# Two half-tiles of tokens in one gather, and their weighted sums through 128x64 diagonals side by side on TensorE

## The reference

```
def peer_ffn(xn, w_query, sub_keys, expert_u, expert_v):
    ...
    idx = i1 * PEER_N_KEYS + i2
    g = jax.nn.softmax(cv, axis=-1)
    ...
    def block(args):
        xb, ib, gb = args
        hid = jax.nn.gelu(jnp.einsum('td,thkd->thk', xb, expert_u[ib]).astype(jnp.float32), approximate=False)
        return jnp.einsum('thk,thkd->td', (gb * hid).astype(xb.dtype), expert_v[ib])
```

## Time and profile before

| | |
|---|---|
| median of 3 runs | 4050.73 us (4046.65 to 4053.82) |
| span of the profiled execution | 5878.7 us |
| its own time beside the span | none is given |
| instructions | 40315 |
| mean granted TensorE clock | 0.555 |
| busy: TensorE, VectorE, ScalarE, GpSimd | 5726, 2887, 1648, 1285 us |
| moved by DMA | 1444 MB, 246 GB/s over the span |

### The profile page before, as it was taken

How to read it: one execution, slowest core, us unless ns; L and a number is a source line. 1 busy time by engine, 2 the same in 40 slices (tenths; PEclk the granted TensorE clock), 3 DMA queues, 4 the chain that set the end, 5 groups by cost and what they waited for, 6 DMA issues and landing times.

```text
span 5878.7 us, 40315 instructions
## 1 busy us (share of the span) xinstructions
PE 5726.4 (97%) x13374; PEld 2787.7 (47%) x13374; DVE 2887.4 (49%) x5745; ACT 1648.5 (28%) x4216; POOL 1285.3 (22%) x1094
## 2 busy tenths in 40 slices
PE   9999999999999998999999999899999999899999
PEld 5555555444444545444445545344445555222222
DVE  3321003665555455756555555756555554744443
ACT  3431101344422211244432211245422211222222
POOL 0000000222222221322222221322222221334343
PEclk6555555555555555555555555555555555555555
DMA  4222222767777775767777775777777775899997
GB/s 155 93 102 81 73 90 95 267 238 266 261 275 268 274 280 202 285 245 280 273 272 297 283 291 190 280 256 271 271 268 308 281 290 191 315 350 342 345 342 281
DMA packets 212948, 1444.45 MB, mean 246 GB/s; under 512 B 27256, under 2 KB 27256, under 8 KB 46340
## 3 DMA queue, kind: packets, MB, share of 16 engines
q0 software_dynamic: 164976, 1133.94, 52.0%
q1 hardware_dynamic: 47632, 307.80, 14.4%
q10 hardware_dynamic: 132, 0.12, 0.0%
HBM read 1439.31 MB, written 7.13 MB: 246 GB/s over the span
## 4 chain that ended last, share of the span: by engine, by line
PE 96%; DVE 2%; ACT 1%; issue 1%; DMA 0%; SPq 0%; ACTq 0%; DVEq 0%
PE banks L609 52%; PE sums L871 21%; PE banks L871 7%; PE banks L748 5%; PE banks L827 3%; PE banks L669 2%; PE banks L736 1%; PE banks L786 1%; PE banks L778 1%; PE banks L694 1%; PE banks L844 1%; DVE x L1479 1%; DVE rows L1470 0%; PE banks L637 0%; PE banks L700 0%
## 5 line engine op out<-in xcount | busy, mean ns | idle before, releaser
L609 PE MATMUL banks<-hT,ring 128*128 128x256 f32 x6656 | 2608.4, 583 | 4.7 <-DVE arena L1316 3.9
L609 PEld LDWEIGHTS banks<-hT,ring 128*128 128x128 f32 x6656 | 1507.5, 228 | 1151.7 <-issue 734.0
L576 POOL DMA_INDIRECT rows<-in_w_uv,idx x1024 | 1237.6, 1209 | 3600.3 <-PE sums L871 1981.3
L1470 DVE CUSTOM_DVE_ANT_0 rows<-rows,xn 128x1024 f32<-128x1024 f32 x1024 | 1241.6, 1220 | 530.8 <-DMA rows<-in_w_uv,idx 528.0
L871 PE MATMUL sums<-rows,diag 128*128 128x512 f32 x1612 | 1285.2, 970 | 70.0 <-ACT diag L1076 47.9
L1479 DVE SCALAR_TENSOR_TENSOR x<-rows,wgt,x 128x1024 f32<-128x1024 f32 x493 | 632.0, 1282 | 234.8 <-ACT wgt L1068 234.0
L871 PEld LDWEIGHTS sums<-rows,diag 128*128 128x128 f32 x1612 | 369.2, 232 | 791.7 <-issue 683.2
L1281 DVE SCALAR_TENSOR_TENSOR arena<-banks,pr,arena 128x254 f32<-128x254 f32 (+1 forms) x512 | 246.8, 482 | 354.6 <-ACT arena L965 340.9
L1063 ACT ACTIVATE gelu<-hid 128x2 f32<-128x2 f32 x512 | 102.9, 201 | 1100.7 <-DVE hid L1470 1099.3
L609 PE MATMUL banks<-yT,ring 128*128 128x256 f32 x1024 | 400.2, 582 | 0.0
L871 PE MATMUL banks<-rows,diag 128*128 128x512 f32 x512 | 393.7, 966 | 0.0
(11 more groups left out here) (205 smaller groups left out, 2955.8 us busy)
## 6 DMA issues: line engine op xcount, KB each, us to landing
ring<-in_w_ssd SPq DMA_DIRECT2D x96, 1024.0 KB, 5.4
ring<-in_w_att SPq DMA_DIRECT2D x64, 1024.0 KB, 6.1
ring<-in_w_mrg SPq DMA_DIRECT2D x52, 1024.0 KB, 8.4
arena<-a_rows POOLq DMA_DIRECT2D x32, 1024.0 KB, 7.6
ring<-in_w_qry SPq DMA_DIRECT2D x32, 1024.0 KB, 4.8
arena<-bias_tiles POOLq DMA_DIRECT2D x16, 1152.0 KB, 7.3
ring<-in_w_out SPq DMA_DIRECT2D x16, 1024.0 KB, 7.0
rows<-in_w_uv,idx POOLq DMA_INDIRECT x1024, 6.8
```

The source lines that it names most:

```text
L576: nc.gpsimd.indirect_dma_start(out=rows[n % NB][:, :], out_offset=None, in_=w_uv, in_offset=bass.IndirectOffsetOnAxis(ap=idx[:, t, s:s + 1 ...
L609: mm = pe.matmul(out, w[:, k * P:(k + 1) * P], rhs[:, k0 + k, :], start=start and k == 0, stop=stop and k == n - 1)
L1470: v.tensor_tensor_reduce(u, u, xn2[:, (n // SLOTS_T) % 3, :], 1.0, 0.0, ALU.mult, ALU.add, hid[:, k:k + 1]).then_inc(u_done, 1)
```

## The change

Tokens are dealt differently over partitions. A gather used to bring one slot of a tile's 128 tokens. Now slots go in pairs, and gather q of a pair (q = 0, 1) brings both slots for 64 tokens, those of half q of the tile: partitions 0 to 63 have one slot, 64 to 127 another (its index is 8 further in the head). So `idx`, `gate` and the normalized x (`xn2`) are laid out by half: `xn2` holds each half's 64 tokens twice, once on each half of the partitions. VectorE writes each half's own copy (`own_rows`) and ScalarE the other (`copies`). The second tile's copies are made in the ssd stage of the next pass (`late_rows`). The norm weight is loaded straight into `xn2` by half tiles, without the wait for the finished x.

The dot product stays one VectorE instruction of 128x1024 a gather. The sum of a pair is now four matmuls, for each 512 columns two: the diagonal is 128x64, two 64x64 diagonals stacked, so that both slots of a token are added in the contraction, and gather q goes to output partitions 64q to 64q + 63. No sum is on VectorE any more. The sum of a pair stands at the even tick k, for slots k - 4 and k - 3. `hid`, `gelu` and `wgt` shrink to 16 columns, `DIAGS` goes from 5 to 6. Gathers are as many and as large as before.

```diff
-BESIDE = [("norm", 0, 1, 8, 60), ("ssd", 0, 2, 22, 80), ("ssd", 2, GROUPS, 70, 50), ("att", 0, 4, 65, 15), ("mrg", 0, 8, 42, 5),
-          ("out", 0, 1, 11, 0), ("norm2", 0, 1, 5, 100), ("query", 0, 2 * PH + 1, 13, 0), ("route", 0, REST, 20, 100)]
+BESIDE = [("norm", 0, 1, 8), ("ssd", 0, 2, 22), ("ssd", 2, GROUPS, 68), ("att", 0, 4, 68), ("mrg", 0, 8, 47),
+          ("out", 0, 1, 11), ("norm2", 0, 1, 5), ("query", 0, 2 * PH + 1, 12), ("route", 0, REST, 15)]
...
-    return list(range(SLOTS_P - LAG - 1, SLOTS_P)) if k == SLOTS_P - 1 else [k - LAG] if k >= LAG else []
+def sums_at(k):
+
+    if k == SLOTS_P - 1:
+        return list(range((k - LAG) // 2, PAIRS_P))
+    return [(k - LAG - 1) // 2] if k % 2 == 0 and k > LAG else []
...
+    c[:, C_I64:C_I64 + HALF] = i[:, None] % HALF == i[None, :HALF]
...
-        xn2 = sb("xn2", [P, 3, D])
+        xn2 = sb("xn2", [P, 2, 2, D])
...
-        diag = [sb(f"diag{n}", [P, P]) for n in range(DIAGS)]
+        hid = sb("hid", [P, HID])
+        diag = [sb(f"diag{n}", [P, HALF]) for n in range(DIAGS)]
...
-                yield place("norm2", 0, 0.2)
-                pool.wait_ge(x_mid.sem, x_mid.at(m, 2))
-                pool.dma_start(n2b, w_n2[m // 2].partition_broadcast(P)).then_inc(n2_in.sem, 16)
+            def norm_rows(m, t):
+
+                for q in range(2):
+                    pool.dma_start(xn2[HALF * q:HALF * q + HALF, t, q, :],
+                                   w_n2[m // 2].partition_broadcast(HALF)).then_inc(n2_in.sem, 16)
...
                     for h in range(2):
-                        mm = pe.matmul(sum_banks(p, t)[:, h, :], diag[e % DIAGS][:, :],
-                                       rows[n % NB][:, D + 512 * h:D + 512 * h + 512], start=q == mine[0], stop=q == mine[-1])
+                        for q in range(2):
+                            mm = pe.matmul(sum_banks(p, t)[HALF * q:HALF * q + HALF, h, :], diag[(2 * n + q) % DIAGS][:, :],
+                                           rows[(2 * n + q) % NB][:, D + 512 * h:D + 512 * h + 512],
+                                           start=j % PAIRS_T == 0, stop=j % PAIRS_T == PAIRS_T - 1)
                     mm.then_inc(v_pe, 1)
...
+            def copies(m, t):
+
+                act.wait_ge(xn_own.sem, xn_own.at(m, t + 1))
+                for q in range(2):
+                    own, other = HALF * q, HALF * (1 - q)
+                    ins = act.activation(xn2[other:other + HALF, t, q, :], xn2[own:own + HALF, t, q, :], ACT.Copy)
+                ins.then_inc(xn_ok.sem, 1)
...
+                for q in range(2):
+                    act.wait_ge(g_w, n + q)
+                    act.activation(diag[(n - 1 + q) % DIAGS][:, :], stacked, ACT.Copy, scale=wgt[:, c + q:c + q + 1]).then_inc(d_ok, 1)
...
+            def own_rows(m, t, scale):
+
+                v.wait_ge(n2_in.sem, n2_in.at(m, 32 * (t + 1)))
+                for q in range(2):
+                    at = slice(HALF * q, HALF * q + HALF)
+                    ins = v.scalar_tensor_tensor(out=xn2[at, t, q, :], in0=x[at, 2 * (m % 2) + t, :], scalar=scale[at],
+                                                 in1=xn2[at, t, q, :], op0=ALU.mult, op1=ALU.mult)
+                ins.then_inc(xn_own.sem, 1)
...
-                    v.scalar_tensor_tensor(out=xo, in0=rows[before % NB][:, D:], scalar=wgt[:, q:q + 1], in1=xo,
-                                           op0=ALU.mult, op1=ALU.add).then_inc(v_dve, 1)
+                v.tensor_tensor_reduce(u, u, xn2[:, t, q, :], 1.0, 0.0, ALU.mult, ALU.add,
+                                       hid[:, n % HID:n % HID + 1]).then_inc(u_done, 1)
```

More of the change, by code:

```diff
@@ L80 @@
 AHEAD = NB - LAG - 1
-DIAGS = 5
+DIAGS = 6
+HALF = P // 2
+PAIRS_T = SLOTS_T // 2
+PAIRS_P = SLOTS_P // 2
+HID = 16
 BEHIND = 3.0
@@ L103, in part_of @@
     return next(n for n, (m, tile, lo, hi) in enumerate(PARTS) if (m, tile) == (p, t) and lo <= h < hi)
-BESIDE = [("norm", 0, 1, 8, 60), ("ssd", 0, 2, 22, 80), ("ssd", 2, GROUPS, 70, 50), ("att", 0, 4, 65, 15), ("mrg", 0, 8, 42, 5),
-          ("out", 0, 1, 11, 0), ("norm2", 0, 1, 5, 100), ("query", 0, 2 * PH + 1, 13, 0), ("route", 0, REST, 20, 100)]
-LAST_ON_DVE = 3
-EARLY = [("query", 14, 17, 3, 100), ("route", 0, REST, 7, 100)]
+BESIDE = [("norm", 0, 1, 8), ("ssd", 0, 2, 22), ("ssd", 2, GROUPS, 68), ("att", 0, 4, 68), ("mrg", 0, 8, 47),
+          ("out", 0, 1, 11), ("norm2", 0, 1, 5), ("query", 0, 2 * PH + 1, 12), ("route", 0, REST, 15)]
+EARLY = [("query", 14, 17, 3), ("route", 0, REST, 7)]
 FEWER = {"ssd": 4, "att": 4, "mrg": 2}
 def deal(table):
-    return [(AT[phase] + EACH[phase] * (first + (last - first) * (i + 1) / ticks),
-             (i + 1) * percent // 100 > i * percent // 100) for phase, first, last, ticks, percent in table for i in range(ticks)]
-BESIDE_1 = [(name, lo, hi, n - (FEWER.get(name, 0) if lo != 0 or name != "ssd" else 0), q) for name, lo, hi, n, q in BESIDE]
+    return [AT[phase] + EACH[phase] * (first + (last - first) * (i + 1) / ticks)
+            for phase, first, last, ticks in table for i in range(ticks)]
+BESIDE_1 = [(name, lo, hi, n - (FEWER.get(name, 0) if lo != 0 or name != "ssd" else 0)) for name, lo, hi, n in BESIDE]
 DEALT = [deal(EARLY), deal(BESIDE_1)] + [deal(BESIDE)] * (PASSES - 2)
 assert len(DEALT[0]) + len(DEALT[1]) == len(DEALT[2]) == SLOTS_P
[L123 to L126, removed]
+PLAN = [[(0, k, due) for k, due in enumerate(DEALT[0])],
+        [(0, len(DEALT[0]) + k, due) for k, due in enumerate(DEALT[1])]]
+PLAN += [[(m - 1, k, due) for k, due in enumerate(DEALT[m])] for m in range(2, PASSES)]
 EARLY_AT = 12
@@ L537, in decay_rows @@
                     pool.dma_start(aBC.rearrange("p d h t -> p d (h t)"), src).then_inc(bc_in.sem, 16)
+                if m:
+                    yield place("ssd", 0, 0.3)
+                    late_norm_rows(m - 1)
                 yield place("ssd", 0, 0.5)
@@ L966, in mixer @@
                                        scale=pr[:, o + 2:o + 3]).then_inc(c_acc.sem, 1)
+                    if m and g == 1:
+                        yield place("ssd", g, 0.7)
+                        copies(m - 1, 1)
                     if m and g == LATE_STEPS - 1:
```

146 lines of the change are left out of this document (70 added, 76 removed).

## The result

The changed kernel takes 4140.5 us (median of 4 runs, 4135.4 to 4142.2) against 4050.9 for the one before: a ratio of 1.0222, 95% interval 1.0208 to 1.0237. It is slower by 90 us.

What follows compares the result with a forecast made beforehand. At the full clock DMA was taken to bound most of the kernel, VectorE close behind. From 4051 us, 27 for three passes and 18 of a 55 us excess came off: 4006, said as 4005, range 3890 to 4190.

Steps and rivals of the forecast that it cites:

- The timed runs are at the full clock: Whole kernel: the first case, timed runs at 2.4 GHz and not the profile's 0.555, so mostly DMA's.
- pass of 909 us: Third pass of the kernel before: the largest of TensorE, VectorE and DMA time in each stage, added up.
- VectorE's 766 us a pass fall by 210: Passes: sums leave VectorE, leaving about 560 us; largest terms fall 9 us a pass, plus 18 us in all given back.
- A pair costs what one slot costs: Sums on TensorE: four half-width matmuls, two side by side, take one slot's 1.71 us at 2.4 GHz; +62 us a pass.
- 0.15 for the visit: TensorE going in and out of half width: 0.15 us for each of 384 pairs, bounds 0 and 0.2; +19 us a pass.
- TensorE stays under DMA: Att and mrg after the change: TensorE needs 213 us of DMA's 233 in att, 187 of 199 in mrg.
- TensorE becomes the bound: Rival in att and mrg: the added sums make TensorE decide below a granted clock of 0.93; 4150 us, chance 0.20.
- Late gathers: Rival: even slots' sums come one tick later, so gathers have 4 ticks instead of 5; 4084 us, chance 0.12.
- No change: Rival: DMA covers all and the 9 us a pass are within the rate's error; 4051 us, chance 0.13.
- halves don't run together: Rival on TensorE: a pair's two halves run one after the other; over 5000 us timed, chance 0.01.
- ScalarE's diagonals 0.34 us: ScalarE: 1024 diagonals of 128x64 instead of 531 of 128x128, 0.34 us each, +140 us in all, hidden.
- no gain in the last stretch at the full clock: Last pass, only gathers: TensorE's time per slot halves, but at the full clock DMA already set it, so nothing.

Runs made afterwards that it cites:

- r9: Kernel before with VectorE's sums done on 8 of their 1024 columns, nothing put on TensorE: 3973.7 us, ratio 0.9807.
- r6: Changed kernel with the sum of a pair one tick earlier, so each buffer is free sooner: 4145.1 us, ratio 1.0236.
- r5: Kernel before with half of the att and mrg sums on TensorE, as single full-width slots: 4111.3 us, ratio 1.0150.
- r4: Changed kernel with half of the output columns of nearly all sums left out on TensorE: 4080.4 us, ratio 1.0071.
- r2: Changed kernel with the tick counts by stage of the kernel before: 4144.5 us, ratio 1.0237.
- r10: Changed kernel with two pairs summed per visit to half width, only for ticks 104 to 223 (about att and mrg): 4128.3 us, ratio 1.0188.
- r7: Changed kernel with two pairs summed per visit to half width everywhere, at every fourth tick: 4189.6 us, ratio 1.0341.
- r1_base: Kernel before, unchanged, run again for a profile at the full clock: 4043.8 us.

## Why the prediction was wrong

It said 4005, faster than 4051. Measured are 4140: inside its range of 3890 to 4190, but on the other side. Step by step:

1. *The timed runs are at the full clock, and DMA bounds att and mrg there.* Right: clocks of 0.94 to 0.95 in every timed run of the kernel before, 416 and 425 GB/s, 71% of mrg's chain. Its pass of 909 us measured 914; that these are so close is in part luck, since the stages in it were cut wrongly (4.) and the rate was too low.
2. *VectorE's 766 us a pass fall by 210, and this frees time.* Right, and too cautious in size: I gave 9 + 6 us a pass for it, r9 shows 25 (76 us over the kernel).
3. *A pair costs what one slot costs, 1.71 us at 2.4 GHz, and 0.15 for the visit.* The first half is right: two 64-column records start 7 ns apart, and a step of the two takes 429 ns, as one of full width does. The price of the visit was too low: 0.35 us at the full clock, above the upper bound of 0.2 that I gave. In the trace ahead of the prediction, at a clock of 0.555, the same count over all steps around the heads gives 0.21 (median of ten), so in that trace a part of the price didn't show. The Trainium skill ("TensorEngine Tiling (Array Packing)", Key Properties) says that a change of tiling mode drains TensorE. The trace agrees that it costs, with 0.14 us on the way in and 0.20 on the way out, each less than the 0.38 us that a record of 256 columns lasts.
4. *TensorE stays under DMA: 213 of 233 us in att, 187 of 199 in mrg.* **This step failed.** Measured are 232 busy of 244, and 176 of 176, while DMA would need, at 425 GB/s, 222 us for att's 94.4 MB and 166 for mrg's 70.4. Four terms of it were mis-sized.
   - *The rate.* I took 400 GB/s for the limit, from a range whose upper end, 427, stood in the earlier trace rows: 11 us too many for DMA in att and 12 in mrg.
   - *The ends of the stages.* The stretches of the earlier trace rows don't end where the stages do. The trace has the last product of att (L786) and the first projection of mrg (L609) at 3256 us, not at 3223, and mrg's end at 3481. So 33 us of att were counted as mrg. With the right ends mrg has 64 MB and 125 us of TensorE at 2.4 GHz, where I had 74 and 148. By my own terms for the change, that is 164 us of TensorE against 162 of DMA at 427 GB/s: no room at all.
   - *The bytes.* At the full clock mrg of the kernel before had 56.5 MB, not 64: what a stage takes in changes with the clock. And the change brought it 13.9 MB more, where I had 5 gathers, 5.2 MB. The two nearly cancel.
   - *TensorE's own load.* In att the kernel before has 194 us busy at a clock of 0.94, which is 183 at the full one, where I had 172; and the visits cost 20 us in the two stages, not 9.

   So the room of 32 us in the two stages was not there. The rows for the ends, of the execution that the earlier trace rows are from: TensorE around 3256, and busy time by stretch as there, for att and mrg with their true ends:

```profile
3251.81 4.71 PE L786 MATMUL banks<-arena 128*64 128x256 f32 x24
3256.46 5.93 PE L609 MATMUL banks<-hT,ring 128*128 128x256 f32 x15
...
2935.00:3256.50 321.50, 317.73 (x865) 158.41 (x863) 179.09 (x266) 92.48 (x241) 87.09 (x70) 0.55 0.74 283
3256.50:3481.00 224.50, 224.50 (x583) 131.16 (x582) 109.53 (x153) 52.83 (x109) 52.94 (x42) 0.56 0.76 284
```

5. *The rival "TensorE becomes the bound", 4150, decides from a granted clock under 0.93.* The mechanism and its place were right. Its condition was wrong: 400 us of TensorE against 432 of DMA should have read 408 against 388. By that it happens at the full clock (0.98 to 1.00 in the two stages), and it should have been the forecast. Its price, 4150 against 4140 measured, was worked out from a clock of about 0.89 that no timed run had: that it came so near is luck.
6. *Late gathers* (4084): VectorE's waits for gathers did grow, 514 to 913 us, but r6 took back 251 of them for nothing, and r9 has 880 in a faster kernel. *No change* and *halves don't run together* fell.
7. *ScalarE's diagonals 0.34 us, VectorE near 2270, ScalarE near 1810, no gain in the last stretch at the full clock.* Measured 0.340, 2323, 1716, and 7 us gained.

The balance of a pass, by the shortfalls: att +17, mrg +10 and out to query +6, against -6 in ssd and -3 in route and norm. Shown by a run: that TensorE's load alone produces mrg's loss and, at 10 us less of it, over a third of att's, and makes the whole 61 us slower (r5), that its removal returns mrg's (r4), and that VectorE's relief alone is a gain (r9). Not settled is the rest of att's loss. Most of it stays when TensorE is relieved (r4), is not due to the counts or to the sum's tick (r2, r6), and a part of it goes with fewer visits (r10: 22 to 16). What remains of the change there is that buffers come free two at a time, and the visits, each of which holds up what stands behind it by 0.35 us; no run tells the two apart, since r7 and r10 change both. Nor was a mixture tried, pairs for one tile of a pass and the old sums for the other. No version that computes everything beat the kernel before.

## What to carry to other kernels

When two engines stand close, moving work pays only up to the second engine's limit in the very stage where it lands, so write for each stage the second engine's load beside the transfer time at the *best* rate the trace shows, since a rate taken too low makes room that isn't there. Find where a stage ends by its first and last instruction before counting its bytes: here 33 us of one stage, counted as the next, made a room of 12 us that wasn't there. Take the bytes and slots of a stage only from an execution in the regime of the timed runs: when a profile is 1.45 times as long as they are, stages have shifted against each other, and scaling one engine's time does not put them back. Read the price of a switch over a whole period, from one steady step to the next: reading its first steps alone gave 0.19 us for 0.35. A long wait on an engine is a price only if that engine ends last: VectorE's 900 us of waiting for gathers stood in the changed kernel and in the fastest one alike.

## What the runs showed of the hardware

- **A DMA share near 1 is not a full rate.** Mrg shows 1.01 at 425 GB/s in `r1_base` and 1.00 at 400 in the changed kernel, 1.00 at 399 in r5. The Trainium skill says that for DMA utilization of HBM, rather than occupancy, is to be read ("Perfetto Trace Analysis", Identifying the Most-Contended Engine); the trace agrees.
- **Going to half width for a pair and back costs TensorE 0.35 us.** At the full clock, f32, 128x64 between records of 128x128: 0.14 us on the way in and 0.20 on the way out, the same in 33 of 34 visits between projections in att and mrg of the changed kernel (the other one holds a wait). Full-width sums between the same records, in r5, cost nothing extra.
- **In the profiles at the full clock, the mean falls where TensorE has less to do.** Granted 0.75 in the last stretch after the change (TensorE busy 0.55) against 0.96 before (0.72), and 0.858 over the whole of r4. The stretch did not get longer, since gathers set it.
- **One program, two regimes.** The same kernel was profiled at 0.555 over 5879 us and at 0.946 over 4042. No profile made later was like the first, and what held the clock at 0.555 stays open.
